# Layer 1's experts with 176 dense and 80 gathered tokens instead of 192 and 64

## The chip, the core and the metric

The kernel runs on one core of a Trainium2 chip. The metric is the device time in microseconds from launch to end, as the median of several runs. The engines are PE (TensorE, matmuls; PEld is its weight load), DVE (VectorE), ACT (ScalarE), POOL (GpSimd) and SP (SyncE, which here only issues DMAs).

## What is computed

Two layers of a trunk over 256 context and 256 latent tokens of width 1024. Each layer has a token mixer and then PEER: for every token and each of 8 heads, the 16 best of 128 x 128 single-neuron experts are found by product keys, and the token's output is the gated sum over its 128 picks. Layer 1 computes only the 256 latent tokens. The change concerns PEER alone (D_MODEL is 1024, PEER_NKEYS 128):

```python
def _peer(h, w_q, sub_keys, expert_u, expert_v):
    ...
        qr = (tb @ w_q).reshape(t, PEER_HEADS, 2, half)
        s = jnp.einsum('thsk,hsnk->thsn', qr, sub_keys).astype(jnp.float32)
        top_s, top_i = lax.top_k(s, PEER_TOPK)
        ...
        gate = jax.nn.softmax(best_s, axis=-1)
        act = jax.nn.gelu(jnp.einsum('td,thkd->thk', tb, expert_u[idx]).astype(jnp.float32),
                          approximate=False)
        w = (gate * act).astype(tb.dtype)
        return jnp.einsum('thk,thkd->td', w, expert_v[idx])
```

## The kernel before

The kernel is written in stages, and every engine's instructions are written out in order by hand, with semaphores between them; no scheduler moves anything. Layer 1 ends with the stages route (queries, scores, top-k), gates, experts and final.

**Two ways to the same sum.** The first 192 latent tokens of layer 1 are *dense*: all 16384 experts pass through TensorE as 128 units of 128 experts. A unit is 1 MB: its u half (512 KB) and its v half (512 KB), loaded by SP into one of 4 slots of the tile `ring`. PE multiplies the u half with the dense tokens `h2b` (`up`: 8 matmuls with 192 columns, float32, which the profile shows as 16 records), ACT takes the gelu into `actB`, DVE multiplies with the gates `gateB` and splits the product into a high and a low float32r part (`wB`), and PE multiplies these with the v half (`down`: 10 matmuls with 512 columns). For `down`, ACT copies the v half into `ehi` and DVE writes the rest into `elo`; both copies have two buffers, so ACT copies unit k once `down(k - 2)` is through. The last 64 tokens are *gathered*: 64 times POOL starts an indirect DMA that fetches 128 rows of 8 KB (u and v of one pick of 64 tokens, in two halves of the partitions) into one of two buffers `gbuf`; DVE forms the dot products with the tokens `h2n` (line 2846, `dot`), ACT takes gelu and gate (lines 2171 and 2172), and DVE adds the v rows to `yg` (line 2856, `add_row`).

**The experts stage.** It runs in turns of 4 units (RING), 32 in all, the last of them unrolled. PE's order is `up(k + 1)`, `down(k)`. DVE's order in step k is: `dot` (k even), `elo`, `add_row` (k odd), gate multiplication, high part, two low parts. A gather is issued by POOL when `add_row` of the gather two before it is done. For the first 20 turns (AHEAD) `up` of the turn's first unit has been done earlier, 14 of them in the route stage and 6 in the gates stage, as chunks of one matmul for each group; their results lie in `act_ahead` and `act_more`. These are the *early* turns, with 3 `up` each; the 11 turns after them are the *late* turns, with 4.

**The gates stage.** In groups of four tokens (48 groups), DVE and POOL, helped by ACT, write one-hot rows into `hot` (4 buffers: a buffer is written again when PE is through with the group four before), and PE multiplies them to a 128 x 128 gate table for each token, which ACT copies into `gateB`. DVE and ACT handle two groups at a time. POOL starts gathers 0 and 1 before its fifth group, and before the stage's first group it moves the picks of the second half of the gathered tokens with two small DMAs (`gidx`, `gval`, line 924).

**The final transposition.** PE brings `yout` and `yg` back to columns per token in 8 steps (line 1623 and two matmuls through the helper `mm`, line 969), then DVE, ACT and PE form the last norm.

## Time and profile before

| | us |
|---|---|
| median of 3 runs | 2748.15 (2742.96 to 2749.76) |
| the profiled execution's own time | 2748.51 |
| its span, first to last instruction | 2746.7 |
| gates stage of layer 1 | about 2089 to 2150 |
| its early turns | about 2154 to 2494 |
| its late turns | about 2494 to 2710 |
| last turn, transposition, final norm | to 2746.7 |

The profile's times are microseconds from the first instruction. "Busy" of PE is time in which a matmul was under way. A row of the timeline gives start, duration, engine, line, operation, operands and count; in square brackets stands how long the engine had been idle before it and what released it. A row that merges n instructions lasts from the first start to the last end.

### The profile page before, as it was taken

What the parts mean: (1) busy time and instruction counts of PE and PEld (TensorE: products, weight loads), DVE (VectorE), ACT (ScalarE), POOL (GpSimd) and SP (SyncE); (2) the same over time, 40 slices, a digit from 0 to 9 for tenths busy, and PEclk for the clock granted to TensorE, in tenths of its full rate; (3) what the DMA queues carried; (4) which work ended last, traced back from release to release, by engine and by line L of the source; (5) the groups of instructions that cost most, each with busy time, mean ns of one, the idle gap of its engine ahead of it and who ended that gap; (6) DMA issues with size and microseconds to landing.
All of it is one profiled execution on the core that took longest, in us unless ns stands there. A gap on an engine that the chain in (4) does not pass through costs nothing.

```text
span 2746.7 us, 48607 instructions
## 1 busy us (share of the span) xinstructions
PE 2625.8 (96%) x16791; PEld 2279.9 (83%) x16791; DVE 2259.3 (82%) x4474; ACT 1200.0 (44%) x2189; POOL 476.5 (17%) x428
## 2 busy tenths in 40 slices
PE   7999999888899999999999999999999999999998
PEld 5878887566788888888888887888979888888887
DVE  6478664999899999999999997797789877777676
ACT  5234442226854444444444445334526533333333
POOL 0000000003532333333332330000004211111010
PEclk9999999887999999999999999999999999999999
DMA  6523322554499999999999994333444699999985
GB/s 269 227 79 103 119 77 107 217 196 163 145 348 366 386 388 388 388 388 385 381 366 369 361 362 154 113 129 112 160 161 134 243 337 333 340 343 332 322 320 210
DMA packets 172367, 708.89 MB, mean 258 GB/s; under 512 B 17088, under 2 KB 50528, under 8 KB 124896
## 3 DMA queue, kind: packets, MB, share of 16 engines
q1 hardware_dynamic: 134480, 431.60, 42.5%
q0 software_dynamic: 37776, 275.83, 27.1%
q8 instruction: 68, 1.11, 0.2%
q14 instruction: 43, 0.35, 0.0%
HBM read 690.61 MB, written 16.65 MB: 257 GB/s over the span
## 4 chain that ended last, share of the span: by engine, by line
PE 84%; DVE 8%; DMA 4%; ACT 3%; issue 2%; SPq 0%; DVEq 0%; ACTq 0%
PE ps L969 83%; DMA ring<-in_w_mod 2%; DMA ring<-in_w_front 1%; DMA gate_scratch<-spill 1%; DVE hot L2803 1%; DVE elo L2274 0%; DVE hot L2800 0%; DVE loP L2343 0%; DVE gst L2498 0%; PE ps L1129 0%; DVE hot L2796 0%; DVE rs L2234 0%; ACT hiP L1672 0%; DVE topi L2685 0%; DMA mcst<-in_mixer_consts 0%
## 5 line engine op out<-in xcount | busy, mean ns | idle before, releaser
L894 POOL DMA_INDIRECT gbuf<-in_expert_rows,gidx x192 | 277.1, 1443 | 1095.7 <-DVE yg L2856 1079.0
L969 PE MATMUL ps<-h2a,ehi 128*128 128x320 f32 x2048 | 453.0, 309 | 0.0
L2186 ACT ACTIVATE ehi<-ring 128x1024 fp32r<-128x1024 f32 x256 | 271.1, 1059 | 396.3 <-PE ps L969 353.0
L2868 DVE TENSOR_TENSOR elo<-ring,ehi 128x1024 fp32r<-128x1024 f32 x256 | 313.6, 1225 | 138.9 <-ACT ehi L2186 136.3
L969 PE MATMUL ps<-ehi,wA 128*128 128x512 f32 x1280 | 376.5, 392 | 3.5 <-DVE wA L2903 3.5
L969 PE MATMUL ps<-h2b,ring 128*128 128x192 f32 x2048 | 358.9, 326 | 1.2 <-ACT act_ahead L2059 1.2
L969 PEld LDWEIGHTS ps<-h2a,ehi 128*128 128x128 f32 x2048 | 347.7, 188 | 10.3
L969 PEld LDWEIGHTS ps<-h2b,ring 128*128 128x128 f32 x2048 | 337.3, 190 | 10.7 <-issue 1.5
L969 PE MATMUL ps<-h2a,elo 128*128 128x320 f32 x1024 | 316.4, 309 | 0.0
L969 PEld LDWEIGHTS ps<-ehi,wA 128*128 128x128 f32 x1280 | 235.5, 188 | 53.8 <-DVE wA L2903 3.7
L2846 DVE SCALAR_TENSOR_TENSOR gbuf<-gbuf,h2n 128x1024 f32<-128x1024 f32 x192 | 234.1, 1219 | 27.2 <-DMA gbuf<-in_expert_rows,gidx 21.2
L969 PE MATMUL ps<-ehi,wB 128*128 128x512 f32 x768 | 250.5, 411 | 0.9 <-DVE wB L2903 0.9
L2856 DVE SCALAR_TENSOR_TENSOR yg<-gbuf,gw,yg 128x1024 f32<-128x1024 f32 x192 | 245.3, 1278 | 0.0
L969 PE MATMUL ps<-elo,wA 128*128 128x512 f32 (+1 forms) x768 | 239.3, 392 | 0.0
L969 PEld LDWEIGHTS ps<-h2a,elo 128*128 128x128 f32 x1024 | 192.8, 188 | 0.0
L969 PEld LDWEIGHTS ps<-ehi,wB 128*128 128x128 f32 x768 | 140.1, 188 | 34.5 <-DVE wB L2903 5.5
L969 PEld LDWEIGHTS ps<-elo,wA 128*128 128x128 f32 (+1 forms) x768 | 131.1, 171 | 38.3
L2197 ACT ACTIVATE actA<-ps 128x320 f32<-128x320 f32 x128 | 56.0, 437 | 237.8 <-PE ps L969 237.8
L969 PE MATMUL ps<-elo,wB 128*128 128x512 f32 (+1 forms) x512 | 159.4, 392 | 0.0
L2813 DVE TENSOR_TENSOR elo<-ring,ehi 128x1024 fp32r<-128x1024 f32 x128 | 155.8, 1217 | 1.9 <-ACT ehi L2152 1.1
L969 PE MATMUL ps<-hot 128*128 128x128 f32 x1024 | 133.8, 281 | 23.2 <-issue 10.2
L969 PEld LDWEIGHTS ps<-hot 128*128 128x128 f32 x1024 | 123.9, 194 | 32.2 <-issue 24.4
(447 smaller groups left out, 4814.4 us busy)
## 6 DMA issues: line engine op xcount, KB each, us to landing
ring<-in_experts SPq DMA_DIRECT2D x512, 512.0 KB, 6.7
ring<-in_w_mod SPq DMA_DIRECT2D x48, 1024.0 KB, 6.7
ring<-in_w_side SPq DMA_DIRECT2D x24, 1024.0 KB, 5.0
ring<-in_w_front SPq DMA_DIRECT2D x12, 1024.0 KB, 7.5
ring<-in_w_merge SPq DMA_DIRECT2D x16, 768.0 KB, 4.3
ring<-in_w_q SPq DMA_DIRECT2D x12, 1024.0 KB, 7.3
gate_scratch<-spill SPq DMA_DIRECT2D x40, 256.0 KB, 2.0
gateA<-gate_scratch SPq DMA_DIRECT2D x16, 640.0 KB, 8.5
```

The source lines that it names most:

```text
L894: pool.indirect_dma_start(gbuf[:, k % 2, :], None, a[f"expert_rows{l}"], bass.IndirectOffsetOnAxis(gidx[:, at:at + 1], 0)).then_inc(gather ...
L969: return pe.matmul(out, w, x, start=start, stop=stop, **k)
L2186: act.activation(ehi[:, 2 + k % 2, :], ring[:, (u + k) % RING, DM:2 * DM], ACT.Copy).then_inc(vhi_ready, 1)
L2197: act.activation(actT[:, k % 2, :], ps[:, 6 + k % 2, 0:dense_tokens(l)], ACT.Gelu).then_inc(act_ready, 1)
L2803: v.tensor_tensor(hot[:, g:g + 2, 0, :, :], row.unsqueeze(1).unsqueeze(1).to_broadcast([P, 2, 4, P]), fours.unsqueeze(3).to_broadcast([P, ...
L2813: v.tensor_tensor(elo[:, r, 0:DM], ring[:, r, 0:DM], ehi[:, k % 2, :].bitcast(F32), ALU.subtract).then_inc(ulo_ready, 1)
L2846: v.scalar_tensor_tensor(rows, rows, 1.0, h2n[:, :], ALU.mult, ALU.mult, accum_out=ga[:, at]).then_inc(dot_ready, 1)
L2856: v.scalar_tensor_tensor(yg[:, :], gbuf[:, n % 2, DM:2 * DM], gw[:, at], yg[:, :], ALU.mult, ALU.add).then_inc(acc_done, 1)
L2868: v.tensor_tensor(elo[:, r, DM:2 * DM], ring[:, r, DM:2 * DM], ehi[:, 2 + b, :].bitcast(F32), ALU.subtract).then_inc(vlo_ready, 1)
```

## The change

176 tokens stay dense (DENSE1) and 16 more (EXTRA) are gathered. So `up` has 176 columns instead of 192; `down` keeps its ten matmuls of 512 columns, with 96 and 48 instead of 128 and 64 weight columns in the last four; gates has 44 groups instead of 48, and the 48 chunks of `up` go one to a group up to group 39 and two to a group in the last four.

The 16 extra tokens have 2048 picks, 16 gathers of 128 rows (8 picks of each token at a time), into one buffer of their own, `gbuf3`. Gather 0 is issued in the gates stage; dot product (`dot_extra`, step 0 of a turn, after `elo`) and sum (`add_extra`, step 2, after `elo`) of the 16 stand in turns 3, 7, 11, 15, 19 and then in each of the 11 late turns 20 to 30. Extra gather j is issued by POOL once `add_extra` of j - 1 is done. ACT's gelu and gate for it stand at the end of step 0 and wait for `dot_extra`. In the gates stage the two small DMAs now stand before POOL's group 12 and the first gathers (three of them) before its group 16, since SP first copies the picks of the extra tokens into `gidx2` and `gval2` with 16 small DMAs (after 18 of the 20 loads ahead).

Added besides: in route one ACT copy of the 16 tokens repeated 8 times (`h2e`), 8 transposes of it on PE and an ACT copy out (`h2x`); a memset of `yg3` on DVE at the start of the experts; a load of the selection matrix `sel` (32 KB) on SP then; at the end six matmuls of bfloat16 on the identity (`keep_on`) and, in each of the 8 steps of the transposition, one matmul more (`yg3` with `sel`). `act_more` goes, its 6 results lie in `act_ahead` too. The loops of DVE and ACT are cut into more pieces (`turns_of`).

```diff
+DENSE1, EXTRA = 176, 16
...
+EXTRA_TURNS = [RING * n + RING - 1 for n in range(AHEAD // RING)] + [AHEAD + n for n in range(EXTRA - AHEAD // RING)]
...
+def turns_of(l):
+    last = NK // RING - 1
+    if l < DEPTH - 1:
+        return ((0, last, None),)
+    early = [x for t in range(0, AHEAD, RING) for x in ((t, RING - 1, None), (t + RING - 1, 1, t // RING))]
+    return (*early, (AHEAD, EXTRA - AHEAD // RING, AHEAD // RING))
...
+                            if j == IN_ROUTE + RING - 1:
+                                sp.wait_ge(gidx_ready, 2)
+                                mine = slice(DENSE1 - P, HALF)
+                                for s in range(P // EXTRA):
+                                    part = slice(EXTRA * s, EXTRA * (s + 1))
+                                    sp.dma_start(gidx2[part, 0:EXTRA], gidx[mine, part]).then_inc(more_in, 16)
+                                    sp.dma_start(gval2[part, 0:EXTRA], gval[mine, part]).then_inc(more_in, 16)
...
                     experts_begin(l)
+                    sp.wait_ge(hot_pool, groups_before(st))
+                    sp.dma_start(sel[:, :], a["pairs"]).then_inc(mcst_in, 16)
...
-                        for t_ in (gidx, gval):
-                            pool.dma_start(t_[0:HALF, first:NK], t_[HALF:P, 0:NK - first]).then_inc(shift_in, 16)
                     pool.wait_ge(pick_col, routes_by(l))
...
-                        if n == (4 if l else 40):
+                        if l and n == 12:
+                            pool.wait_ge(more_in, 32 * SLOTS + 32 * (P // EXTRA))
+                            for t_ in (gidx, gval):
+                                pool.dma_start(t_[0:HALF, first:NK], t_[HALF:P, 0:NK - first]).then_inc(shift_in, 16)
+                        if n == (16 if l else 40):
...
                             for m in range(2):
                                 gather(l, m)
+                            if l:
+                                gather_extra(0)
...
+                        if l and k // 2 - 1 in EXTRA_TURNS[:-1] and k % 2 == 0:
+                            j = EXTRA_TURNS.index(k // 2 - 1) + 1
+                            pool.wait_ge(more_acc, NK // SLOTS + j)
+                            gather_extra(j)
...
+                    if l == DEPTH - 1:
+                        pe.wait_ge(h2d_ready, 3)
+                        for c in range(KD):
+                            last = pe.transpose(ps[:, c // 4, (c % 4) * P:(c % 4) * P + P], h2e[:, c, :], ident)
+                        last.then_inc(more_ps, 1)
...
-                            chunk(IN_ROUTE + n // KD, n % KD)
+                            more = n - (dense_tokens(l) // 4 - KD // 2)
+                            for m in (n,) if more < 0 else (n + more, n + more + 1):
+                                chunk(IN_ROUTE + m // KD, m % KD)
...
                         down(k, NK // RING - 1, k == RING - 1)
-                    if not l:
-                        keep_on(8, 6)
...
+                        pe.wait_ge(more_acc, NK // SLOTS + EXTRA)
...
                             pe.transpose(o[:, 0:P], yout[:, 0, s_], ident)
-                            mm(o[:, P:P + 64], yout[:, 1, s_], pair, True, True)
+                            mm(o[:, P:DENSE1], yout[0:2 * half, 1, s_], pair1[0:2 * half, :], True, True)
+                            mm(o[:, DENSE1:DENSE1 + EXTRA], yg3[:, s_], extra, True, True)
                             last = mm(o[:, P + 64:256], yg[:, s_], pair, True, True)
...
+                            if l and k == 0:
+                                act.activation(h2e[:, :, :].rearrange("p c (s t) -> p c s t", t=EXTRA),
+                                               h2T[:, :, DENSE1:DENSE1 + EXTRA].unsqueeze(2).to_broadcast([P, KD, P // EXTRA, EXTRA]), ACT.Copy
...
+                    if l == DEPTH - 1:
+                        act.wait_ge(more_ps, 2)
+                        act.activation(h2x[:, :], ps[:, 0:2, :].rearrange("p b d -> p (b d)"), ACT.Copy)
...
+                    def gathered_extra(j):
+                        act.wait_ge(more_dot, NK // SLOTS + 1 + j)
+                        at = bass.ds(j, 1)
+                        own.link(act.activation(ga3[:, at], ga3[:, at], ACT.Gelu))
+                        act.activation(ga3[:, at], ga3[:, at], ACT.Copy, scale=gval2[:, at]).then_inc(more_gw, 1)
...
-                                step(k, i, True, first)
...
+                    def dot_extra(j):
+                        dve.wait_ge(more_rows[0], 16 * (NK // SLOTS // 2 + 1) + j * 16)
+                        v.scalar_tensor_tensor(gbuf3[:, 0:DM], gbuf3[:, 0:DM], 1.0, h2x[:, :], ALU.mult, ALU.mult, accum_out=ga3[:, bass.ds(j, 1)]
+                                               ).then_inc(more_dot, 1)
+                    def add_extra(j):
...
+                        dve.wait_ge(more_gw, NK // SLOTS + 1 + j)
+                        dve.wait_ge(acc_zero, 4)
+                        dve.wait_ge(more_acc, NK // SLOTS + j)
+                        v.scalar_tensor_tensor(yg3[:, :], gbuf3[:, DM:2 * DM], ga3[:, bass.ds(j, 1)], yg3[:, :], ALU.mult, ALU.add
+                                               ).then_inc(more_acc, 1)
...
+                        elif extra is not None:
+                            (dot_extra if k == first else add_extra)(i + extra)
...
-                        turns(RING * IN_ROUTE, AHEAD - IN_ROUTE)
-                        turns(RING * AHEAD, NK // RING - 1 - AHEAD)
+                        v.memset(yg3[:, :], 0.0).then_inc(acc_zero, 1)
+                        for first, n, extra in turns_of(l):
+                            turns(RING * first, n, extra)
```

On POOL, from route to the early turns of layer 1 (`gidx<-gidx` and `gval<-gval` are the small DMAs of line 924, `hot` is a group of the gates stage). Before:

```order
L911 MEMSET nth 128x256 x16
L916 DMA x_scratch<-xT 1024x1x256
L924 DMA gidx<-gidx 64x64
L924 DMA gval<-gval 64x64
L939 TENSOR_SCALAR hot<-cst,idxB 128x128 x4
L894 DMA gbuf<-in_expert_rows,gidx 128x2048 x2
L939 TENSOR_SCALAR hot<-cst,idxB 128x128 x44
L894 DMA gbuf<-in_expert_rows,gidx 128x2048 x62
```

On POOL at the same place in the changed kernel (line 930 is `gather_extra`):

```order
L972 TENSOR_SCALAR hot<-cst,idxB 128x128 x12
L959 DMA gidx<-gidx 64x64
L959 DMA gval<-gval 64x64
L972 TENSOR_SCALAR hot<-cst,idxB 128x128 x4
L920 DMA gbuf<-in_expert_rows,gidx 128x2048 x2
L930 DMA gbuf<-in_expert_rows,gidx 128x2048
L972 TENSOR_SCALAR hot<-cst,idxB 128x128 x28
L920 DMA gbuf<-in_expert_rows,gidx 128x2048 x7
L930 DMA gbuf<-in_expert_rows,gidx 128x2048
```

The small DMAs and the first gathers moved behind groups 12 and 16, and a third gather stands with them.

On DVE, step 0 of a late turn (`elo` is the low part of the v half, `actB` the gate multiplication). Before:

```order
L2846 SCALAR_TENSOR_TENSOR gbuf,ga<-gbuf,h2n 128x1024
L2866 ISA
L2868 TENSOR_TENSOR elo<-ring,ehi 128x1024
L2879 REGISTER_ALU
L615 REGISTER_ALU
L2894 ISA
L2894 TENSOR_TENSOR actB<-actB,gateB 128x192
```

The same step in the changed kernel:

```order
L2926 SCALAR_TENSOR_TENSOR gbuf,gaB<-gbuf,h2n 128x1024
L2946 ISA
L2948 TENSOR_TENSOR elo<-ring,ehi 128x1024
L2909 ISA
L2910 ISA
L2910 SCALAR_TENSOR_TENSOR gbuf3,ga3<-gbuf3,h2x 128x1024
L2961 REGISTER_ALU
L632 REGISTER_ALU
L2975 ISA
L2975 TENSOR_TENSOR actB<-actB,gateB 128x176
```

The wait for the extra rows now stands between `elo` and the gated weights that `down` of this unit needs.

## Rows read from the trace of the kernel before

**Rows 1.** The page: shares of the chain that ended last, by engine

```profile
PE 84%; DVE 8%; DMA 4%; ACT 3%; issue 2%; SPq 0%; DVEq 0%; ACTq 0%
```

**Rows 2.** Windows: us; PE, PEld, DVE, ACT, POOL busy; clock, DMA share, GB/s

```profile
900.00:1400.00 500.00, 500.00 (x2781) 446.38 (x2781) 470.00 (x663) 244.64 (x488) 161.60 (x105) 1.00 1.01 386
...
2089.00:2150.00 61.00, 60.38 (x480) 57.88 (x480) 57.01 (x93) 52.01 (x121) 37.32 (x47) 1.00 0.31 104
...
2170.00:2477.00 307.00, 307.00 (x1588) 266.67 (x1587) 244.65 (x470) 110.42 (x198) 33.72 (x36) 1.00 0.93 339
2495.00:2710.00 215.00, 215.00 (x1144) 192.03 (x1143) 150.21 (x287) 70.73 (x132) 21.51 (x22) 1.00 0.90 322
```

**Rows 3.** Timeline of the gates stage, layer 1, and of route ahead of it

```profile
2016.78 0.60 ACT L2023 ACTIVATE qrT<-ps 128x512 f32<-128x512 f32 x1 [6.31 <-PE ps L969]
...
2084.31 0.87 PE L1489 MATMUL ps<-cst,pick 128*128 128x128 f32 x6 [1.92 <-DVE pick L2763]
...
2089.68 1.08 POOL L894 DMA_INDIRECT gbuf<-in_expert_rows,gidx  x1 [0.17 <-issue]
...
2091.05 0.97 POOL L894 DMA_INDIRECT gbuf<-in_expert_rows,gidx  x1 [0.30 <-issue]
...
2120.53 1.05 PE L969 MATMUL ps<-hot 128*128 128x128 f32 x8
...
2121.69 0.79 POOL L939 TENSOR_SCALAR hot<-cst,idxB 128x128 f32<-128x128 f32 x1 [0.43 <-PE ps L969]
...
2122.94 1.22 DVE L2803 TENSOR_TENSOR hot<-ps,idxB 128x1024 f32<-128x1024 f32 x1
...
2124.14 0.69 DVE L2796 TENSOR_TENSOR hot<-ps,idxB 128x512 f32<-128x512 f32 x1
```

**Rows 4.** The tile gateB: its instructions, ns min/median/max, first and last start

```profile
L2102 ACT ACTIVATE gateB<-ps x24: 1023/1023/1025, 2091.6 to 2149.6; 128x1024 f32<-128x1024 f32 x24
...
L2894 DVE TENSOR_TENSOR actB<-act_more,gateB x6: 350/351/351, 2391.7 to 2476.9; 128x192 f32 x6
```

**Rows 5.** Timeline of one early turn: first its step 0, then its step 3

```profile
2338.12 1.23 DVE L2846 SCALAR_TENSOR_TENSOR gbuf<-gbuf,h2n 128x1024 f32<-128x1024 f32 x1
...
2339.43 1.23 DVE L2868 TENSOR_TENSOR elo<-ring,ehi 128x1024 fp32r<-128x1024 f32 x1
...
2339.83 0.30 ACT L2172 ACTIVATE gw<-ga,gval  x1
...
2350.29 2.76 PE L969 MATMUL ps<-h2b,ring 128*128 128x192 f32 x16
2350.55 1.06 ACT L2186 ACTIVATE ehi<-ring 128x1024 fp32r<-128x1024 f32 x1 [1.94 <-PE ps L969]
...
2351.64 1.22 DVE L2868 TENSOR_TENSOR elo<-ring,ehi 128x1024 fp32r<-128x1024 f32 x1 [1.77 <-ACT ehi L2186]
...
2352.78 1.28 DVE L2856 SCALAR_TENSOR_TENSOR yg<-gbuf,gw,yg 128x1024 f32<-128x1024 f32 x1
...
2353.97 0.35 DVE L2894 TENSOR_TENSOR actB<-actB,gateB 128x192 f32<-128x192 f32 x1
...
2354.33 0.94 POOL L894 DMA_INDIRECT gbuf<-in_expert_rows,gidx  x1 [8.85 <-DVE yg L2856]
```

**Rows 6.** Waits of the weight load, early turns: us, times, longest

```profile
PEld ps L969 <- DVE wB L2903: 5.5, 20, 1.2
```

**Rows 7.** Tile gbuf, 2600 to 2727: us from a gather's issue to its landing

```profile
DMA to landing us min/median/max: 6.8/8.9/9.7
```

**Rows 8.** DMA issues, 1200 to 1400 (layer 0): count and median us to landing

```profile
gbuf<-in_expert_rows,gidx POOLq DMA_INDIRECT x28, 9.4
gbufX<-in_expert_rows,gidx POOLq DMA_INDIRECT x14, 10.8
```

**Rows 9.** Timeline of the transposition at the end, one of its 8 steps

```profile
2730.70 0.39 PE L969 MATMUL ps<-cst,yg 128*128 128x64 f32 x2
...
2730.93 0.28 PE L1623 MATMUL ps<-cst,yout 128*128 128x128 f32 x1
```

## What the change will do to the time: the prediction

> **What bounds the kernel now.** I read the page's chain first: TensorE has 84% of it [rows 1]. Then the windows by stage [rows 2]: in the early turns and in the late ones PE is busy all of the time at a granted clock of 1.00 (2.4 GHz), DVE for 80% and 70% and DMA for 93% and 90%, with 339 and 322 GB/s. A late unit has 26 records on PE and a late turn 4 units, so 1144 records in 215 us make 11 turns of 19.55 us. An early turn takes 17.04 us: its gate multiplications with `act_more` start 85.2 us apart over 5 turns [rows 4]. In the gates stage it is different: PE looks busy, but the two-group pace is DVE's. There L2803 is followed by the next pair's L2796 without a gap [rows 3], and the 24 copies into `gateB` start 2.52 us apart (58.0 / 23) [rows 4]; one group's work on PE is 8 x 0.11 + 2 x 0.16 = 1.2 us.
>
> So columns taken from `up` are worth time in the turns, and groups taken from gates are worth DVE's pace. What is added is one more DVE pair of operations for some turns and one more gather, and the question is where they wait.
>
> **What a column is worth.** 16 records of 192 columns last 2.76 us from first start to last end, one alone 0.33, so they start 0.162 us apart [rows 5]; 8 of 128 columns 0.110 apart ((1.05 - 0.28) / 7) [rows 3]. That is 0.81 ns for a column, 13 ns for 16 columns, 0.21 us for an `up` of 16 records. `down` keeps its ten matmuls of 512 columns: nothing, taken at zero, since fewer weight columns don't shorten the stream.
>
> **Gates stage.** Two pairs of groups less: -2 x 2.52 = -5.0. The four chunks that move into the last four groups stand where DVE has no more to do: two records of about 0.15 each, 4 x 0.30 = +1.2. POOL: its `hot` for a group is released when the group four before is through, so three groups, 3.8 us, pass before PE needs it; less its own 0.79 there are 2.9 us of room [rows 3]. Two gathers issued in a row there took 1.37 and 1.0 us [rows 3], so three take 3.4: +0.5. The two small DMAs (as short, before group 12) fit into that room, and so does the wait for the 16 DMAs of SP: the 18th load ahead is issued right after the picks exist, and the next load waits for a ring slot some nine groups later anyway. Sum: **-3.3**.
>
> **Early turns (20).** In step 3 PE waits for DVE: 5.5 us over 20 turns, 0.28 in each [rows 6]. The rows of one such step show the chain: `down` of two units before ends, ACT copies `ehi` at 2350.55, DVE's `elo` 2351.64, `add_row` 2352.78, gate multiplication 2353.97, then the parts of `wB` [rows 5]. This chain does not get shorter with `up`, but for some 0.05 in narrower operations, while PE's way to the same point loses 0.21. So of the 3 x 0.21 = 0.63 of a turn 0.16 turns into a longer wait: 0.465 x 20 = -9.3. In the 5 turns with an extra, step 0 gets one more DVE operation of 1.31 (start to start of `dot` and `elo` [rows 5]). PE comes to this `down` 4.6 us after the last one began (a `down` of 2.4 and an `up` of 2.2); DVE needs 3.6 now (1.31 + 1.15 + 1.17), then 4.9: +0.3 x 5 = +1.5. The rows have landed long before, four turns ahead. Sum: **-7.8**.
>
> **Late turns (11).** PE alone would go from 19.55 to 19.55 - 4 x 0.21 = 18.7. But here the extras form a loop of their own, since `gbuf3` is one buffer: rows land, `dot_extra`, `add_extra` two steps later, next gather, landing. From the start of `dot_extra`: ACT has gelu and gate done after 2.0 (2338.12 to 2340.13) and only then copies `ehi` of step 1, 1.06, so `elo` starts at 3.2; then, from start to start [rows 5], `elo` 1.14, `add_row` 1.19, gated parts 1.12, `dot` 1.31, `elo` 1.14, `add_extra` 1.28 to its end: 10.4. POOL issues 0.27 later (2352.78 + 1.28 to 2354.33) and about 0.1 passes from landing to start. The loop is 10.75 + L, with L the time from a gather's issue to its landing. In the late turns now L is 8.9 in the median, 6.8 to 9.7, with gathers 9.8 us apart [rows 7]. In layer 0 it is 9.4 for `gbuf`, and 10.8 for `gbufX`, which is issued 2 us behind another [rows 8], at 386 GB/s [rows 2]. The extra is issued some 5 us behind gather 2t + 2. I take 9.1, near the late turns' own median, since most of the gather ahead has left the queue by then; both ends, 8.4 and 10.8, stay for the range. The loop is then 19.85, 0.3 more than a turn now: 11 x 0.3 = **+3.3** instead of -9.1.
>
> Transfers: a late turn then moves 7 MB (8 halves of 512 KB, 3 gathers of 1 MB), 7.34 million bytes in 19.85 us, 370 GB/s; layer 0 carries 386 with PE busy all the time [rows 2]. An early turn moves 5.8, every fourth 6.8, about 363 GB/s on average. I count no loss.
> The Trainium skill speaks against this: its page "DMA: Bandwidth & Descriptors", section "Where 436 GB/s comes from", says that for transfers between HBM and SBUF the HBM side binds at some 358 GB/s. By that a late turn would take 20.5 us, an estimate from that page, the mean early turn 16.84, and this sum would come out some 11 us later. The trace's 386 GB/s over 500 us disagrees, and I go by the trace.
>
> **The rest.** Last turn: 4 `up` with 0.21: -0.8. Transposition: one more pair of records with a weight load in each of 8 steps; such a pair takes 0.23 from start to start [rows 9], the one beside it 0.17, so 8 x 0.2 = **+1.6**, with nothing to hide it, as the final norm waits for the last step. Zero: the ACT copy `h2e` lies where ACT waits 6.3 us for the next queries; the 8 transposes and the copy `h2x` (about 1 us each) precede ups whose sum gets 13 x 0.21 = 2.7 shorter, and PE idles 1.92 before it needs the picks [rows 3]; uncovered they would cost 1 us each. `keep_on` lies in PE's wait for the copies of `yout`; memset `yg3` and the load of `sel` stand at the stage's start beside ACT's first copy. More pieces of loops: the seam at which `act_more` begins leaves the 17.04 us as they are [rows 4].
>
> **Sum:** -3.3 - 7.8 + 3.3 - 0.8 + 1.6 = -7.0. From the profiled execution's own 2748.5 that is **2741.5**; that execution lies 0.4 above the median of 2748.15, which makes no difference here. 0.3%, about 8.2 us, is what a measurement of this kernel can tell from no change: 2739.9 and 2756.4 are the borders.
>
> **Rivals.**
> *The extra gather lands soon enough.* If L is 7.9 or less, or the loop overlaps in some way that I don't see, the late turns run at PE's 18.7: -9.1 in place of +3.3, 2729. For it: the shortest landing is 6.8 [rows 7]. Against: the median is 8.9, with less traffic than there will be. 0.12.
> *The extra gather lands as the second one does in layer 0.* With L = 10.8 the loop is 21.55: 11 x 2.0 = +22, 2760, slower than before. It decides from L = 10.5. For it: the same constellation in layer 0 [rows 8]. Against: there it follows 2 us behind another gather, here 5. 0.09.
> *The transfers are the limit.* DMA is at 93% with 339 GB/s in the early turns [rows 2]. Should layer 1 not go beyond some 350, a late turn takes 21.0 (+16) and the mean early turn 17.2 (+3 in place of -7.8): 2765. At 370 nothing is lost. The skill's limit of 358 GB/s, named above, would lie between, by that estimate. Against: the share is 1.01 at 386 GB/s in layer 0, so share does not grow in step with the rate. 0.08.
> *The early turns gain nothing*, because more delayed rows (DVE, ACT) meet the chain of step 3: 2741.5 + 7.8 = 2749. 0.12.
> *The change doesn't do what it says* (a column less saves nothing): records of 128 and 192 columns speak against it; 0.02, 2754.
>
> **How the numbers follow.** My forecast, L between 8.4 and 9.8, gives 2734 to 2749 and has 0.57. Of that 0.25 lies below 2739.9, with the first rival 0.37; slower are the second and third, 0.17; the rest, 0.46, is within 0.3%. The range leaves out half of the first rival and most of the second and third: 2731 to 2757.
>
> **What would show it.** Gates: 22 copies into `gateB`, still 2.52 apart. Starts of `up` records 0.149 apart. Early turns 16.6, with PE's wait before step 3 at 0.4. Late turns 19.85, with one wait a turn of PE for `wB` in step 0 (about 1.1 us), and DVE's `dot_extra` waiting for its DMA; landing of `gbuf3` 9.1. If the late turns are 18.7, the loop is wrong; if DVE waits for `ehi` and ACT for `ring` instead, the transfers are the limit.

## The result, and the profile after

On the same chip: 2746.16 us before (median of 4 runs, 2742.96 to 2749.76) and 2729.11 us after (median of 4 runs, 2724.62 to 2730.45). The ratio is 0.9931, 95% interval 0.9920 to 0.9943: 0.7% faster. Forecast were 2741.5 us and a time within 0.3%, with a range of 2731 to 2757: the time came out 12.4 us below the forecast, just below the range, and on the side to which the prediction had given 0.37. The profiled execution's span went from 2746.7 to 2728.7, by 18.0 us.

First the windows of the changed kernel, with the columns of [rows 2]: layer 0, the gates, the early turns, the late turns.

```profile
900.00:1400.00 500.00, 500.00 (x2787) 446.77 (x2786) 469.67 (x662) 244.53 (x486) 160.06 (x104) 1.00 1.01 385
2089.00:2148.00 59.00, 57.18 (x453) 54.19 (x454) 53.20 (x87) 49.44 (x114) 36.81 (x47) 1.00 0.38 130
2166.00:2468.00 302.00, 301.88 (x1598) 251.27 (x1597) 251.01 (x486) 110.34 (x209) 38.63 (x40) 1.00 0.95 360
2487.00:2694.00 207.00, 207.00 (x1145) 179.25 (x1144) 171.24 (x320) 75.02 (x154) 30.05 (x32) 1.00 0.99 388
```

Read the last one against the last of [rows 2]. TensorE is busy for all of the late turns, as it was; VectorE goes from 150 us in 215 to 171 in 207, and the DMA engines from a share of 0.90 at 322 GB/s to 0.99 at 388. The work that was added is there, and it has gone beside TensorE's.

To see where the 18.0 us are, the experts stage is cut where the first matmul of `down` starts: that of turn 0, of turn 20 (the first late one) and of turn 31 (the last). Timeline of TensorE, before:

```profile
2155.52 0.50 PE L969 MATMUL ps<-ehi,wB 128*128 128x512 f32 x1 [0.94 <-DVE wB L2903]
...
2498.87 0.53 PE L969 MATMUL ps<-ehi,wB 128*128 128x512 f32 x1
...
2714.18 0.53 PE L969 MATMUL ps<-ehi,wB 128*128 128x512 f32 x1
```

And after:

```profile
2151.60 0.50 PE L1007 MATMUL ps<-ehi,wB 128*128 128x512 f32 x1 [1.11 <-DVE wB L2985]
...
2487.36 0.50 PE L1007 MATMUL ps<-ehi,wB 128*128 128x512 f32 x1
...
2694.46 0.52 PE L1007 MATMUL ps<-ehi,wB 128*128 128x512 f32 x1
```

The gates are measured from the transposition of the picks (2084.31 before [rows 3], 2084.79 after), since layer 1's route stage begins at 1997 to 2004 us from run to run, by work that the change leaves as it is.

| stretch | before | after | difference | forecast |
|---|---|---|---|---|
| picks to the first `down` | 71.21 | 66.81 | -4.4 | -3.3 |
| 20 early turns | 343.35 | 335.76 | -7.6 | -7.8 |
| 11 late turns | 215.31 | 207.10 | -8.2 | +3.3 |
| last turn, to its last `down` matmul | 14.4 | 14.2 | -0.2 | -0.8 |
| from there to the end | 18.1 | 19.9 | +1.9 | +1.6 |

With the 0.5 us by which the picks come later this is -18.0. Four of five terms came out within 1.1 us. The late turns alone missed by 11.5 us: 18.83 us a turn, and 19.85 were forecast. So the experiments are about the late turns: does the loop of `gbuf3` exist, and if it does, why does it cost nothing?

The extra gathers of the late turns (GpSimd's line of `gather_extra`: its instructions, who waits for them, landings):

```profile
L930 POOL DMA_INDIRECT gbuf<-in_expert_rows,gidx x10: 939/939/940, 2495.2 to 2664.5; - x10
...
  DVE gbuf L2910: 18.3, 10
...
DMA to landing us min/median/max: 8.2/8.5/9.2
```

One turn of the loop, first on VectorE, then on GpSimd:

```profile
2522.21 1.22 DVE L2910 SCALAR_TENSOR_TENSOR gbuf<-gbuf,h2x 128x1024 f32<-128x1024 f32 x1 [1.55 <-DMA gbuf<-in_expert_rows,gidx]
...
2525.16 1.23 DVE L2948 TENSOR_TENSOR elo<-ring,ehi 128x1024 fp32r<-128x1024 f32 x1 [0.74 <-ACT ehi L2250]
2526.30 1.28 DVE L2936 SCALAR_TENSOR_TENSOR yg<-gbuf,gw,yg 128x1024 f32<-128x1024 f32 x1
2527.50 0.33 DVE L2975 TENSOR_TENSOR actB<-actB,gateB 128x176 f32<-128x176 f32 x1
...
2528.50 1.22 DVE L2926 SCALAR_TENSOR_TENSOR gbuf<-gbuf,h2n 128x1024 f32<-128x1024 f32 x1
...
2529.64 1.22 DVE L2948 TENSOR_TENSOR elo<-ring,ehi 128x1024 fp32r<-128x1024 f32 x1
2530.78 1.28 DVE L2918 SCALAR_TENSOR_TENSOR yg<-gbuf,ga,yg 128x1024 f32<-128x1024 f32 x1
...
2541.10 1.23 DVE L2910 SCALAR_TENSOR_TENSOR gbuf<-gbuf,h2x 128x1024 f32<-128x1024 f32 x1 [1.63 <-DMA gbuf<-in_expert_rows,gidx]
```

```profile
2532.59 0.94 POOL L930 DMA_INDIRECT gbuf<-in_expert_rows,gidx  x1 [3.80 <-DVE yg L2918]
```

`dot_extra` (L2910) waits for its rows in every late turn, `add_extra` (L2918) follows 8.6 us later, and the gather at 2532.59 can't start before `add_extra` has ended, since there is one buffer. From `dot_extra` to the gather's issue pass 10.12 us in most late turns (10.38 in this one), from issue to landing 8.5 in the median, 0.13 from landing to the next `dot_extra`: 18.75 us, and not 19.85. TensorE's own late turn is 18.83. By that reading the loop is closed and without a gap, and lies 0.08 us below TensorE's pace. That is by medians; the slow landings count in the mean, and from the first `dot_extra` of the late turns to the eleventh it is 18.81 a turn. So the two paces are equal as far as this trace can tell, and it takes the experiments to say which of them sets the time. In step 0 the weights are ready 0.05 to 0.6 us ahead of their `down`; before, it was 2.8.

### The profile page after: what moved, and what is told of

It reads as the page before. It is cut to its first block, busy times and chain, and to the rows that moved or that the text cites. A ratio compares the mean times of both kernels' runs of the same rounds, so it can differ in the third digit from the quotient of the medians.

```text
span 2728.7 us, 48609 instructions
## 1 busy us (share of the span) xinstructions
PE 2605.3 (95%) x16789; PEld 2243.3 (82%) x16789; DVE 2283.1 (84%) x4515; ACT 1201.5 (44%) x2213; POOL 489.3 (18%) x440
## 3 DMA queue, kind: packets, MB, share of 16 engines
HBM read 707.42 MB, written 16.65 MB: 265 GB/s over the span
## 4 chain that ended last, share of the span: by engine, by line
PE 82%; DVE 8%; DMA 4%; ACT 3%; issue 2%; POOL 0%; SPq 0%; DVEq 0%; ACTq 0%
PE ps L1007 82%; DMA ring<-in_w_mod 2%; DMA ring<-in_w_front 1%; DMA gate_scratch<-spill 1%; DVE elo L2340 0%; DVE hot L2869 0%; DVE loP L2409 0%; DVE gst L2564 0%; PE ps L1167 0%; DVE rs L2300 0%; DMA ring<-in_w_merge 0%; ACT hiP L1720 0%; DMA ring<-in_experts 0%; DVE hot L2866 0%; DVE elo L2352 0%
## 5 line engine op out<-in xcount | busy, mean ns | idle before, releaser
L1007 PE MATMUL ps<-h2b,ring 128*128 128x176 f32 x2048 | 332.4, 313 | 2.2 <-ACT act_ahead L2114 2.2
L1007 PEld LDWEIGHTS ps<-h2b,ring 128*128 128x128 f32 x2048 | 315.8, 191 | 15.1 <-issue 2.5
L1007 PE MATMUL ps<-ehi,wB 128*128 128x512 f32 (+1 forms) x768 | 255.1, 414 | 1.3 <-DVE wB L2985 1.1
L1007 PEld LDWEIGHTS ps<-ehi,wB 128*128 128x128 f32 (+1 forms) x768 | 132.0, 180 | 44.1 <-DVE wB L2985 9.0
```

Of the source, the lines that this page charges most:

```text
L1007: return pe.matmul(out, w, x, start=start, stop=stop, **k)
```

## The experiments

In each of them three numbers are read: the length of the 11 late turns between the first `down` of turn 20 and that of turn 31; A, from the start of `dot_extra` to the issue of the next gather (most frequent value; the range where there is none); and L, issue to landing (median; a dash where the trace can't pair most of them). Of first_16_turns A and L are those of its first 16 turns. All times of whole runs are medians; the first four kernels ran on one chip beside the same runs of the kernel before, and the two groups of four behind them likewise, so that times of different groups are compared by their ratio to the kernel before: 0.001 of it is 2.7 us, and two ratios can be told apart from about 0.002.

| run | us | ratio to before (interval) | 11 late turns | A | L |
|---|---|---|---|---|---|
| after_again | 2728.5 | 0.9935 (0.9922 to 0.9948) | 207.6 | 10.12 | 8.5 |
| add_after_w2 | 2751.4 | 1.0020 (1.0011 to 1.0029) | 228.0 | 11.25 | 9.3 |
| add_after_w1 | 2727.4 | 0.9932 (0.9919 to 0.9945) | 206.5 | 7.8 to 8.4 | - |
| first_16_turns | 2760.8 | 1.0056 (1.0043 to 1.0069) | 207.1 | 10.11 | 8.6 |
| no_extra | 2726.3 | 0.9928 (0.9915 to 0.9942) | 207.1 | | |
| add_after_gate | 2743.2 | 0.9982 (0.9974 to 0.9991) | 222.1 | 10.90 | 9.4 |
| row_after_w3 | 2732.4 | 0.9953 (0.9941 to 0.9966) | 208.7 | 10.13 | 8.7 |
| moved_three | 2726.9 | 0.9931 (0.9917 to 0.9944) | 207.1 | 7.85 | - |
| memset_2 | 2733.6 | 0.9953 (0.9939 to 0.9966) | 213.5 | 10.52 | 8.7 |
| memset_10 | 2760.2 | 1.0041 (1.0027 to 1.0055) | 239.8 | 12.12 | 9.7 |
| half_loads | 2746.5 | 0.9995 (0.9985 to 1.0004) | 220.2 | 11.25 | 8.6 |
| no_yg3_pair | 2726.7 | 0.9926 (0.9913 to 0.9940) | 208.2 | 10.12 | 8.5 |

### The changed kernel again

> The changed kernel once more, as the base that the other runs are set against on the same chip. Both theories: 2729 us, about 17 below the kernel before; early turns 16.67, late turns 18.83 each.

2728.5 us, a ratio of 0.9935. The late turns took 207.6 us, one after the other 19.29, 18.85, 18.79, 18.88, 18.79 and then 18.83; the turn ahead of them 19.99. In those long ones the extra had landed late (L of 9.9 and 9.05) and TensorE waited for `wB` in step 0. So the loop does touch TensorE now and then: 1 to 2 us in this execution.

### The loop made longer by moving `add_extra`

In `step`, the add of the extra goes behind the weight block of step 2:

```
-                            (dot_extra if k == first else add_extra)(i + extra)
+                        elif extra is not None and k == first:
+                            dot_extra(i + extra)
 ...
                         last.then_inc(w_ready, 1)
+                        if extra is not None and k == first + 2:
+                            add_extra(i + extra)
```

> add_extra stands behind the weight block of step 2 and no longer ahead of it; the work is the same. Loop theory: in the late turns the single buffer gbuf3 closes a loop of 10.12 (start of dot_extra to the next gather's issue) + about 8.5 (issue to landing) + 0.13 = 18.76 us, just under the 18.8 of TensorE. One weight block, 1.0 us, makes it 19.8, so 10 to 11 late turns get 1.0 longer: +10 us on the changed kernel (2739), and the wait shows in step 0 of each late turn. Rival (TensorE alone sets the pace, the landing adapts and has some us in reserve): 0, within 1 us, late turns still 18.83.

+22.9 us, as much as the late turns grew (228.0 less 207.6 is 20.4) and some early ones beside them. No work was added, and TensorE now waits. Waits of the weight load in the late turns of this run, where the changed kernel has one of 0.5 us in after_again and none in its own profile:

```profile
PEld ps L1007 <- DVE wB L2985: 17.9, 10, 2.5
```

A + L + 0.14 is 20.7 us; the turns took 228.0 / 11 = 20.73. The loop is real and binds as soon as it is longer than TensorE's turn. The size was off, though, by a factor of two: A grew by 1.13, about as expected, but L grew too, by 0.8 us:

```profile
L930 POOL DMA_INDIRECT gbuf<-in_expert_rows,gidx x10: 936/1677/1680, 2496.5 to 2684.0; - x10
...
DMA to landing us min/median/max: 8.7/9.3/9.9
```

The gather's own instruction on GpSimd took 1.68 us here, where it takes 0.94 in the changed kernel. That looked like the cause, and add_after_gate, below, was made to try it.

### The loop made shorter

The same move, but `add_extra` behind the weight block of step 1 (`k == first + 1`).

> add_extra stands behind the weight block of step 1, half a turn earlier than now (one dot and one elo, 2.4 us, earlier); the work is the same. Loop theory: the loop is shorter by 2.4 us (if the landing stays at 8.5; with 10.8, as of a second gather 2 us behind another in layer 0, it is about the same as now), TensorE's own 18.8 stays the bound: 0 to -0.5 us on the changed kernel, and the room between the weights of step 0 and their down rises from 0.05-0.6 to about 2 us. Rival (the loop costs something in the late turns even now): up to 0.04 x 11 less per turn, -0.5; rival that TensorE has no bound of its own at 18.8: -10 or more.

2727.4 us against 2728.5, well inside the intervals: no difference that can be told. The late turns are 18.77 each, all alike, and the weights of step 0 are ready 0.3 to 2.2 us early. So an `add_extra` 2.3 us earlier gives nothing back: what bounds the late turns is TensorE. The gather now follows 2.2 us behind another, and is slower for it; the issues on GpSimd:

```profile
2582.49 0.94 POOL L920 DMA_INDIRECT gbuf<-in_expert_rows,gidx  x1 [8.45 <-DVE yg L2936]
2584.68 1.68 POOL L930 DMA_INDIRECT gbuf<-in_expert_rows,gidx  x1 [1.25 <-DVE yg L2918]
```

The first seven extras of the experts stage, which the trace pairs with a landing, took 9.6 to 11.5 us, median 9.9; in the late turns 9.9 to 11.6 us pass from an extra's issue to the next `dot_extra`, median 10.5. Five of these `dot_extra` still waited for their rows, 3.3 us in all, and TensorE never for `wB`. For such a place only the 10.8 of the second gather in layer 0 stood in the trace of before [rows 8]. The price that the prediction's second rival put on a gather close behind another is about right; its premise, that the extra of the changed kernel would land like that, is not (8.5).

### The extras in the first 16 turns

```
-EXTRA_TURNS = [RING * n + RING - 1 for n in range(AHEAD // RING)] + [AHEAD + n for n in range(EXTRA - AHEAD // RING)]
+EXTRA_TURNS = list(range(EXTRA))
 ...
+    return ((0, EXTRA, 0), (EXTRA, AHEAD - EXTRA, None), (AHEAD, last - AHEAD, None))
```

> The 16 extra rows lie in turns 0 to 15, one in each, in place of five early ones and the first 11 late ones. Loop theory: the loop (9.94 + 8.4 + 0.1 = 18.5) is longer than an early turn (16.67), so turns 1 to 15 take 18.5: 15 x 1.8 = 27, less some 1.3 of room at the start, +26 us on the changed kernel (2755); late turns without an extra stay at TensorE's 18.8, so nothing comes back. Rival (no loop; an extra costs only its operations): 11 turns with an extra more at +0.05 to +0.3: +1 to +3 us.

+32.3 us. This is the clearest of the runs, because TensorE's own early turn, 16.67, is far below the loop. The first `down` of turn 0 and that of turn 15:

```profile
2147.25 0.50 PE L1006 MATMUL ps<-ehi,wB 128*128 128x512 f32 x1 [2.26 <-DVE wB L2984]
...
2430.16 0.50 PE L1006 MATMUL ps<-ehi,wB 128*128 128x512 f32 x1 [0.35 <-DVE wB L2984]
```

282.91 us for 15 turns, 18.86 each; the loop's terms in this run are 10.11 + 8.6 + 0.12 = 18.83. The turns follow the landings one by one (18.55 to 19.26). Turns 16 to 18, without an extra, took 16.67, and the late turns 18.83 each with 2.7 us of room in step 0. So the same extra that costs 2.2 us in an early turn costs nothing in a late one. The expected +26 used an A of 9.94, as the five spaced extras have it, and not 10.11; that makes 3 of the 6 us, and the rest is L (8.6 and not 8.4) and that no room at the start was left.

### No extras at all

Here the 16 gathers, `dot_extra` and `add_extra` are left out; everything else stays.

> The 16 extra gathers, their dots and adds are left out (the experts of 16 gathered tokens are then missing from the result); 176 dense columns, the gates and the transposition stay. Loop theory: the extras cost only the jitter of the loop, late turns at 18.83 instead of a mean of 18.87 and turns 19, 20 at 18.83 instead of 19.99 and 19.29 in the last profile: 1 to 2 us below the changed kernel, 2727. The room before the down of step 0 goes to 2.7 us, as in the late turns without an extra of the run with the first 16 turns. Rival (the extras cost TensorE or the transfers a share of every turn): 5 us or more.

A ratio of 0.9928 against 0.9935, which the intervals don't tell apart. Late turns 18.83 each, early ones 16.67, both as with the extras, and the weights of step 0 are ready 2.7 us early. Windows of the early and the late turns:

```profile
2151.00:2487.00 336.00, 336.00 (x1781) 280.06 (x1781) 268.66 (x523) 123.00 (x223) 37.59 (x40) 1.00 0.94 346
2487.00:2694.00 207.00, 207.00 (x1145) 179.43 (x1144) 148.04 (x287) 71.41 (x132) 20.57 (x21) 1.00 0.91 330
```

18.83 is TensorE's own pace, at 330 GB/s as at 388. Early and late turns together take 542.6 us here, 542.9 in the first profile of the changed kernel and 544.7 in after_again: all 16 extras cost 0.3 to 2.1 us there.

### A smaller step, and the length of the gather's instruction

`add_extra` behind the gate multiplication of step 2, ahead of the copy into `wB`:

```
                             link(v.tensor_tensor(w_, from_, g, ALU.mult))
+                            if extra is not None and k == first + 2:
+                                add_extra(i + extra)
                             link(v.tensor_copy(wh[:, b, :], actT[:, b, :]))
```

> add_extra stands behind the gate multiplication of step 2 and ahead of the copy into wB: 0.35 us later than now. In add_after_w2 the loop grew by 2.0 and not by 1.0: the gather's own instruction on GpSimd took 1.68 us there in place of 0.94, as VectorE had a long operation running when it began. Theory that the instruction's length goes with the long operation beside it: here short operations run beside it, so 0.94 stays, the loop is 18.87 + 0.35 = 19.2 on average, +0.35 x 11 = +4 us on the changed kernel (2732.5). Rival (landing grows with any delay, since the next gather follows more closely): 19.6 or more, +8.

By the ratios it is +13 us on the changed kernel (0.9982 against 0.9935): the theory had +4, its rival +8 or more. Part of it was my sum: A grew by 0.78 and not 0.35, since `add_extra` now stands behind the wait for the end of the multiplication (0.29 us of idle time in the row) on top of the 0.34 of the multiplication itself:

```profile
2597.70 1.28 DVE L2918 SCALAR_TENSOR_TENSOR yg<-gbuf,ga,yg 128x1024 f32<-128x1024 f32 x1 [0.29 <-DVE actB L2975]
```

The other part is L again, and the gather's instruction is as short as in the changed kernel:

```profile
L930 POOL DMA_INDIRECT gbuf<-in_expert_rows,gidx x10: 936/948/948, 2496.4 to 2679.2; - x10
...
DMA to landing us min/median/max: 8.3/9.4/9.8
```

So L can grow to 9.4 with that instruction at 0.95 us, and its length is not needed to explain the landings; what part it has in add_after_w2 is not separated. A + L + 0.14 = 20.4, turns 20.2: the loop's sum holds again.

What sets the instruction's length can be read from the rows. In add_after_w1 this operation of VectorE runs when the gather of 2584.68 begins, and ends at 2585.55; the gather's instruction ends at 2586.36, 0.81 us later:

```profile
2584.33 1.22 DVE L2926 SCALAR_TENSOR_TENSOR gbuf<-gbuf,h2n 128x1024 f32<-128x1024 f32 x1
```

It is so in the experts stage of all twelve traces of a kernel with extras, for `gather` and `gather_extra` alike: each of the some 100 gathers that began while a 1.2 us operation of VectorE had been running for 0.07 us or more ended 0.80 to 0.82 us after that operation, and so took 1.4 to 2.0 us in place of 0.94.

### The gather alone held back

GpSimd writes some columns that nobody reads ahead of each gather of a late turn, N times, N = 2 and N = 10; no other engine's order is touched:

```
                             pool.wait_ge(more_acc, NK // SLOTS + j)
+                            if j > AHEAD // RING:
+                                for m in range(N):
+                                    pool.memset(gval2[:, EXTRA:NK // SLOTS], 0.0).then_inc(nth_ready, 1)
+                                    pool.wait_ge(nth_ready, DEPTH + N * (j - AHEAD // RING - 1) + m + 1)
                             gather_extra(j)
```

> Ahead of each gather of an extra for the late turns GpSimd does two small memsets (128x48, to columns that nobody reads), an estimate of 0.2 each; no other engine's order changes. Fixed-landing theory: the loop goes from 18.87 to 18.87 + 0.4 = 19.3, times 11, +4 us on the changed kernel (2732.5). Bunching theory (once the loop holds TensorE up, the loads that it releases crowd around the extra gather and its landing goes from 8.5 to 9.3, as in add_after_gate): 20.0, +13 us (2741).

> Ten such memsets, an estimate of 2 us, ahead of each gather for the late turns. Both theories have the loop in it one to one, so that this gives the slope: fixed landing 8.6: 18.87 + 2.0 = 20.9, +22 us (2751); landing 9.3 as in add_after_gate: 21.6, +30 us (2759). If the landing gets shorter as the transfers have more time (share of DMA below 0.95): 20.3, +16 us.

With N = 2, A is 10.52, 0.40 longer, L is 8.7, and the turns take 213.5 / 11 = 19.41 (sum: 19.36): 0.54 above the 18.87 of after_again, 5.9 us over the late turns, +5 us in all by the ratios. The loop has no reserve: a delay of 0.4 us that stands in GpSimd's order alone shows in the late turns (213.5 us, where the kernels with an undelayed `add_extra` have 207.1 to 208.7). That speaks for a landing that stays, and against the idea that it jumps to 9.3 as soon as the loop binds. With N = 10, A is 12.12, L 9.7 and the turns take 21.80 (sum 21.96): 32 us over the late turns, +29 us in all by the ratios, the upper one of the expectation's figures. Here L did grow, in spite of a lower load of 336 GB/s. The landings for N = 2, then those for N = 10:

```profile
L930 POOL DMA_INDIRECT gbuf<-in_expert_rows,gidx x10: 946/946/2008, 2490.4 to 2665.6; - x10
...
DMA to landing us min/median/max: 8.3/8.7/10.0
...
L930 POOL DMA_INDIRECT gbuf<-in_expert_rows,gidx x10: 946/1754/1910, 2494.6 to 2692.4; - x10
...
DMA to landing us min/median/max: 7.9/9.7/10.6
```

A turn thus grows by more than the delay: with A longer by 0.40 (N = 2), 0.78 (add_after_gate), 1.13 (add_after_w2) and 2.00 us (N = 10), the turns are longer by 0.54, 1.32, 1.86 and 2.93.

TensorE's clock is a second thing that could lengthen them. With N = 10 the granted clock over the late turns is 0.97 (read by pieces of 20 us, it is 0.91 to 0.94 in five of eleven, since it fell to its lower level, 1.2 GHz, for a part of them, and 1.00 in the rest), and with add_after_w2 it is 0.98. The columns are those of [rows 2]:

```profile
2487.00:2700.00 213.00, 192.69 (x1023) 164.21 (x1022) 152.19 (x283) 65.89 (x136) 47.68 (x130) 0.97 0.90 336
```

But with N = 2, in add_after_gate and in half_loads it stays at 1.00 and the turns are longer all the same, and where it falls they are still as long as the loop's sum, in which TensorE has no term.

### Less traffic beside the gather

As add_after_w2, and in the late turns only the first half of the columns of the four weight halves for `up` is loaded (the rest of the tile keeps old values):

```
+                w = DM // 2 if l and i is not None and k > RING * AHEAD else DM
-                sp.dma_start(ring[:, e % RING, 0:DM], src[:, 0:DM]).then_inc(u_in[e % RING], 16)
+                sp.dma_start(ring[:, e % RING, 0:w], src[:, 0:w]).then_inc(u_in[e % RING], 16)
```

> As add_after_w2, and in the late turns only the first 512 of 1024 columns of the four upper halves (the weights of up) are loaded, 256 KB each in place of 512; the rest of the tile keeps old values, so the result misses that part. 6.3 million bytes a turn in place of 7.3. Traffic theory (the landing of the extra depends on what the loads of SyncE move beside it): it falls from 9.4 to about 8, the loop of 11.25 + 8 + 0.1 = 19.4, 1.4 x 11 = 15 us under add_after_w2 (2736). Rival (the landing is the gather's own, or set by the other gathers around it): 2751, still 9.4.

L falls from 9.3 to 8.6 (8.0 to 9.4 over ten gathers, where it was 8.7 to 9.9), and the late turns from 20.73 to 20.02; A is the same. By the ratios it is 7 us under add_after_w2, half of what the traffic theory said and more than its rival's nothing. 14% less to transfer takes 0.7 us from a landing that takes 9.3. The traffic beside a gather is part of L, but not all of the difference between places.

### A move that should have won, and did not

The early turns lose 0.25 us each in step 3, where `down` waits for `wB`. The add of step 3 goes behind the weights:

```
                         elif k % 2:
-                            add_row(k // 2, i)
+                            if not late_row(k, first):
+                                add_row(k // 2, i)
 ...
                         last.then_inc(w_ready, 1)
+                        if late_row(k, first):
+                            add_row(k // 2, i)
```

(`late_row` is true in step 3 of a turn below 20 of layer 1.)

> In the early turns add_row of step 3 stands behind the weight block. Step theory (the chain ehi, elo, add_row, gate, wB holds PE up by 0.25 in each early turn): step 3 gets 1.15 us of room, early turns 16.67 become 16.41, 20 x 0.26 = -5 us on the changed kernel (2723.5); in the five turns after, with an extra at step 0, some of it may be lost (dot_extra behind add_row, up to 0.4 x 5 = +2). Rival (16.67 is TensorE's own pace there): 0.

The chain of step 3 was right: undisturbed turns took 16.42 to 16.44 and no longer 16.67. But the ratio is 0.9953 against 0.9935 for the changed kernel, at the edge of what can be told, and by the traces nothing is won: 338.6 us for the early turns (335.8 and 337.1 in the two profiles of the changed kernel) and 208.7 for the late ones. The gather that waits for this add now goes out 1.2 us later, and `dot` of the next step 2 waits for it. Waits in the early turns, the changed kernel:

```profile
DVE gbuf L2926 <- DMA gbuf<-in_expert_rows,gidx: 9.6, 12, 1.6
...
PEld ps L1007 <- DVE wB L2985: 9.0, 19, 1.4
```

and with the add moved:

```profile
DVE gbuf L2926 <- DMA gbuf<-in_expert_rows,gidx: 49.0, 19, 3.5
...
PEld ps L1007 <- DVE wB L2990: 4.5, 9, 0.7
```

TensorE's wait is halved, and VectorE's for rows is five times as long; turns of 16.5 to 17.4 and one of 21.0 on the way to the late turns eat the gain. It is the same kind of loop once more, that of the two buffers `gbuf`.

> Three moves at once, no work changed: add_row of step 3 behind the weights in the early turns; dot_extra of the five early extras behind the weights of step 0 (its gate on ScalarE in step 1); add_extra behind the weights of step 1 everywhere. Theory: early turns 16.41 in all 20 (-5), late turns at 18.77 with 1 to 2 us of room in step 0 (-1 to -2 for the jitter of the loop): 2722. Rival (other waits move in): 2727.

With `dot_extra` and `add_extra` moved as well it is 2726.9 us, a ratio of 0.9931 against 0.9935 for the changed kernel: undisturbed early turns of 16.42, 20 of them in 335.5 us all the same, and late ones of 18.83. None of these versions beats the changed kernel by more than can be measured.

### The matmul of `yg3` at the end

Left out is the matmul that transposes the 16 columns of the extras.

> The matmul of yg3 in each of the 8 steps of the last transposition is left out (the 16 columns of the gathered extras are then missing from the result). The trace gives such a step 0.73 us with it and 0.51 without: 8 x 0.22 = -1.8 us on the changed kernel (2726.8). Rival (it is hidden beside the copies): 0.

From the last `down` to the end 18.17 us, in place of 19.94: the pair costs 1.77 us and nothing hides it. In the whole run the ratio falls by 0.0009, 2.5 us, less than the intervals can tell. A step of the transposition in the changed kernel:

```profile
2711.33 0.28 PE L1670 MATMUL ps<-cst,yout 128*128 128x128 f32 x1
2711.45 0.32 PE L1007 MATMUL ps<-sel,yout 96*128 96x48 f32 x2
2711.61 0.36 PE L1007 MATMUL ps<-sel,yg 128*128 128x16 f32 x2
2711.81 0.41 PE L1007 MATMUL ps<-cst,yg 128*128 128x64 f32 x2
2712.07 0.28 PE L1670 MATMUL ps<-cst,yout 128*128 128x128 f32 x1
```

0.74 us from transpose to transpose, of which the pair with `sel,yg` takes 0.20.

## Why the prediction was right, and where it was wrong

**What a column is worth: right.** Early turns went from 17.05 to 16.67 and late ones from 19.55 to 18.83, that is 0.38 and 0.72 us; 0.465 and, for four `up`, 0.84 were forecast with 0.21 for an `up`. The late turns give 0.18 for an `up`, and 3 x 0.18 less the 0.16 of the longer wait is the 0.38 of an early turn: one size, 15% too high, makes both differences.

**Gates: right in kind, 1.1 us too careful.** The copies into `gateB` are 22 and no longer 24 [rows 4]:

```profile
L2157 ACT ACTIVATE gateB<-ps x22: 1024/1024/1026, 2092.0 to 2145.7; 128x1024 f32<-128x1024 f32 x22
```

They are 2.56 apart and were 2.52, 0.8 us over 21 gaps. Some 0.5 of it is the third gather, as forecast: the two copies around the gathers come 2.80 and 2.70 after the ones before them, and 2.39 and 2.60 in no_extra, which issues two there. One of these waits, in group 16:

```profile
2110.07 1.13 PE L1007 MATMUL ps<-hot 128*128 128x128 f32 x8 [0.35 <-POOL hot L972]
```

Of the +1.2 for the chunks that moved into the last groups some 0.5 came: the last gap between copies is 2.98 and was 2.44. From the last copy to the first `down` it was 5.95 us and is 5.90. The transposes, `h2e` and `h2x` were taken at zero and are: from the first query copy of the route to the picks 81.16 us before and 81.17 after.

**Early turns: right in sum (-7.6 for -7.8), through two errors that cancel.** An undisturbed turn gained 0.38 and not 0.465, 1.7 us less in all. The +0.3 for each of the five turns with an extra did not come: four took 16.65 to 16.80, and turn 19, which leads over to the late ones, 18.94 for the 18.83 that it takes without extras. VectorE needs 4.74 us there from one weight block to the next, as forecast with 4.9, but TensorE comes not 4.6 us after the last `down` began but 4.86, so that the extra operation fits by a tenth of a microsecond.

**Late turns: the step that failed.** The prediction set 10.75 + L, L = 9.1, against TensorE's 18.7 and took the loop. The loop is there as described, gap-free, in every late turn, but it lasts 18.75:

- 10.75 was 10.25 (A 10.12 and 0.13 from landing to `dot_extra`). The pieces were taken from start to start in an early turn [rows 5], where `dot` to `elo` had a wait in it (1.31; now 1.14), the weight block was wider (1.12; now 1.00) and `ehi` later. Each is off by a tenth or two and all in one direction.
- L was 8.5 and not 9.1. The prediction took it near the 8.9 of other gathers, 9.8 us apart [rows 7]; 4.5 us behind one gather and 3.3 to 4.4 ahead of the next it is shorter, although there is more traffic. The trace of before had no row for such a place.
- TensorE's turn was 18.83 and not 18.7.

Of the 1.1 us between 19.85 and 18.75 half is A and half is L; TensorE's 18.83 leaves 1.02 of it, and that times 11 is 11.2 of the 11.5 us that the late turns missed by. So the step that failed is the loop's length in the prediction's sum: its mechanism was right, two of its terms, A and L, were half a microsecond too long each, and the longer of the two paces was TensorE's 18.83 and not the loop's 19.85. The first rival (landing soon enough, TensorE's pace, 2729) had the time right. It decides at L of 7.9 by the prediction's numbers; with the measured A and TensorE's 18.83 it is 8.6, and L has its median at 8.5. A forecast that takes the difference of two sums of 19 us has to carry the error of both: half a microsecond in each was within what the rows could tell, and by that the case was open. A chance of 0.12 for the rival was too low for it.

**Transfers: right.** 388 GB/s over 207 us in the late turns, and 390 in the add_after_w1 run, where TensorE was not held up. The page "DMA: Bandwidth & Descriptors" of the Trainium skill, section "Where 436 GB/s comes from", which the prediction weighed, would have capped this at 358 by the sentence taken from it; these runs disagree with it for this kernel. But the share is 0.99 to 1.00, and row_after_w3 shows that gathers are no longer early enough once the turns get shorter. So I expect that the next thing to be taken off TensorE here would meet the loops of the gathers and the transfers; no run tried it.

**The end: right.** +1.9 and +1.6 forecast; 1.77 of it is the `yg3` pair, as the run without it shows. The last turn gained 0.2 and not 0.8, since in its step 3, which has no `up` ahead, `wB` is ready only 0.15 us before its `down` in both kernels.

**Left open.** Why L differs between places: 8.5 (changed kernel), 8.6 (first 16 turns), 8.7 (N = 2), 9.3 to 9.4 (`add_extra` in or behind the weights of step 2), 9.7 (N = 10), 9.9 (2.2 us behind another gather). It is not the length of the instruction on GpSimd alone (9.4 with 0.95 us), and not the mean load: it was 8.5 at 388 GB/s and 9.7 at 336. Nor is it only how closely the next gather follows, the rival in add_after_gate's expectation: that was 2.9 us in add_after_gate and with N = 2 alike, and L was 9.4 and 8.7. Less traffic took 0.7 us off. What crowds in just then was not separated.

## What to carry to other kernels

A buffer that is gathered into, read and gathered into again closes a loop: use, last use, issue, landing. Add its terms and set the sum beside the bound engine's time for the same period; below it the gather was all but free here, above it every microsecond cost 1.35 to 1.7, since the landing got longer too, wherever in the loop it was spent, even on GpSimd, which is 85% idle. Here the two sums could be read to about 1 us in 19, and that was more than lay between them: in such a case give both outcomes real chances, and take the terms from rows in the stage itself, less the waits that are in them. If it is to be safe, shorten the loop on purpose: moving the last use 2.3 us earlier cost nothing and gave step 0 most of its room back (0.3 to 2.2 us of 2.7).

## What the runs showed of the hardware

- One core moved 388 to 391 GB/s over 200 us, from weight loads of 512 KB and gathers of 1 MB together, at a DMA share of 0.99 to 1.00. TensorE stayed at the full granted clock, 1.00, and lost nothing by it: 18.83 us a turn at 330 and at 388 GB/s.
- A gather's own instruction on GpSimd took 0.94 us in most places and 1.4 to 2.0 in others with the same work. Where a 1.2 us operation of VectorE was already running when it began, it ended 0.8 us after that operation, in some 100 cases without an exception (begun within 0.04 us of each other, they went either way). This is read from rows, and no run was made to try it.
- Where TensorE had to wait for `wB` in the late turns, its granted clock fell to 1.2 GHz at times in some kernels and not in others: over 2487 to 2700 us it was 0.98 in add_after_w2 with 17.9 us of waits of the weight load, 0.97 with N = 10 and 22.5 us, but 1.00 in add_after_gate with 16.0 us.
- From issue to landing a gather of 128 rows of 8 KB took 8.5 us in the median in one place and 9.9 in another with equal traffic per turn; a loop that was costed with one number for it was costed to a microsecond at best.
